# Interleaving the first gate and up weight quarters of a two-layer hybrid decoder step, and storing its last two output tiles singly

## The reference

```
x <- LN1(alpha*x + 0.5*SwiGLU_1(x))
x <- LN2(alpha*x + W_o( sum_b sigmoid(g_b(x)) * y_b(x) ))
x <- LN3(alpha*x + 0.5*SwiGLU_2(x))
_swiglu(x, wg, wu, wd) = (silu(x @ wg) * (x @ wu)) @ wd        # D_FF = 2816
```

## Time and profile before

| | |
|---|---|
| median of 3 runs | 1395.87 us (1395.16 to 1395.97) |
| the profiled execution | 1396.94 us, of which its span is 1395.0 us |
| instructions | 25447 |
| PE busy | 1376.8 us (99%), 10566 matmuls |
| DVE busy | 898.0 us (64%) |
| ACT busy | 667.2 us (48%) |

### The profile page before, as it was taken

The page is one execution under the profiler, slowest core; times in us unless marked ns, Lnnn a source line. Parts: engine busy times, 40 slices in busy tenths (PEclk is TensorE's granted clock), DMA queues, the critical chain, the costliest instruction groups (busy, mean ns, idle before and its releaser), DMA issues.

```text
span 1395.0 us, 25447 instructions
## 1 busy us (share of the span) xinstructions
PE 1376.8 (99%) x10566; PEld 1356.7 (97%) x10566; DVE 898.0 (64%) x1180; ACT 667.2 (48%) x896; POOL 35.0 (3%) x68
## 2 busy tenths in 40 slices
PE   8999999999999999999999999999999999999996
PEld 8999999999899999999999999999998999999996
DVE  5555558486965885554685555686887568655444
ACT  5444446445444664444474444463544355644433
POOL 0100000000101000000000000000001000000000
PEclk9999999999999999999999999999999999999999
DMA  6554444654656454444445544445465453554441
GB/s 237 204 180 155 148 167 164 223 181 172 232 190 212 162 182 160 170 158 161 166 167 179 180 156 149 166 165 198 166 240 197 166 201 122 181 180 153 171 166 57
DMA packets 39997, 243.60 MB, mean 175 GB/s; under 512 B 4576, under 2 KB 4592, under 8 KB 16368
## 3 DMA queue, kind: packets, MB, share of 16 engines
q1 hardware_dynamic: 33264, 219.00, 45.2%
q0 software_dynamic: 5936, 22.01, 4.3%
q10 hardware_dynamic: 720, 1.47, 0.3%
HBM read 238.97 MB, written 3.50 MB: 174 GB/s over the span
## 4 chain that ended last, share of the span: by engine, by line
PE 92%; DVE 5%; DMA 1%; ACT 1%; issue 1%; DVEq 0%
PE ps L438 29%; PE ps L437 29%; PE ps L439 29%; DVE wlo L1026 1%; DMA raw<-in_w_in 1%; PE ps L525 1%; PE ps L629 1%; PE ps L652 1%; PE ps L597 0%; PE ps L636 0%; ACT whi L729 0%; PE ps L469 0%; DMA raw<-in_ffn_wg 0%; PE ps L470 0%; PE ps L474 0%
## 5 line engine op out<-in xcount | busy, mean ns | idle before, releaser
L1026 DVE TENSOR_TENSOR wlo<-raw,whi 128x1024 fp32r<-128x1024 f32 (+1 forms) x450 | 510.4, 1141 | 314.6 <-ACT whi L729 310.7
L729 ACT CAST whi<-raw 128x1024 fp32r<-128x1024 f32 (+1 forms) x446 | 438.1, 987 | 496.5 <-PE ps L439 397.6
L437 PE MATMUL ps<-xh,whi 128*128 128x288 f32 (+1 forms) x2144 | 635.9, 297 | 1.2 <-DVE xl L1225 1.2
L438 PE MATMUL ps<-xl,whi 128*128 128x288 f32 (+1 forms) x2144 | 631.4, 294 | 0.0
L439 PE MATMUL ps<-xh,wlo 128*128 128x288 f32 (+1 forms) x2144 | 630.5, 294 | 0.0
L437 PEld LDWEIGHTS ps<-xh,whi 128*128 128x128 f32 x2144 | 404.5, 189 | 3.6 <-DVE xl L1225 1.6
L438 PEld LDWEIGHTS ps<-xl,whi 128*128 128x128 f32 x2144 | 406.2, 189 | 0.8
L439 PEld LDWEIGHTS ps<-xh,wlo 128*128 128x128 f32 x2144 | 405.5, 189 | 0.0
L437 PE MATMUL ps<-hh,whi 128*128 128x288 f32 (+1 forms) x1088 | 322.2, 296 | 0.0
L438 PE MATMUL ps<-hl,whi 128*128 128x288 f32 (+1 forms) x1088 | 319.4, 294 | 0.0
L439 PE MATMUL ps<-hh,wlo 128*128 128x288 f32 (+1 forms) x1088 | 319.2, 293 | 0.0
(11 more groups left out here) (185 smaller groups left out, 750.5 us busy)
## 6 DMA issues: line engine op xcount, KB each, us to landing
raw<-in_w_in SPq DMA_DIRECT2D x48, 1024.0 KB, 4.9
raw<-in_ffn_wg SPq DMA_DIRECT2D x43, 1024.0 KB, 4.9
raw<-in_ffn_wu SPq DMA_DIRECT2D x43, 1024.0 KB, 4.8
raw<-in_ffn_wd SPq DMA_DIRECT2D x32, 1024.0 KB, 4.9
raw<-in_ffn_wd SPq DMA_DIRECT2D x16, 768.0 KB, 4.2
pool<-in_cache_k POOLq DMA_DIRECT2D x16, 512.0 KB, 4.3
pool<-in_cache_v POOLq DMA_DIRECT2D x16, 512.0 KB, 6.2
raw<-in_w_o SPq DMA_DIRECT2D x8, 1024.0 KB, 4.9
```

The lines of the kernel that those rows point to most:

```text
L437: mm(out, wh, mh, start=start, stop=False)
L438: mm(out, wh, ml, start=False, stop=False)
L729: s_.copy(whi[:, s, k0:k1, :], raw[:, s, k0:k1, :]).then_inc(hi_ready, 1)
L1026: return v.tensor_tensor(out, full, high.bitcast(F32), sub)
```

## The change

It does five things.

1. SP issues the two first blocks by turns in quarters: gate 0, up 0, gate 1, up 1 and so on, 8 issues of 256 KB in place of 4 of 256 KB and 2 of 512 KB. Each up quarter has a semaphore of its own (`second_in`).
2. ACT no longer casts the first x quarter; DVE does (`first_xh`). ACT casts gate quarter c, x quarter c (from c = 1) and up quarter c by turns; DVE computes `wlo` of the gate quarter, `xl`, and `wlo` of the up quarter by turns.
3. PE multiplies gate quarter c and then up quarter c. Within a quarter it does the four `whi*xh` matmuls, the four `wlo*xh` and the four `whi*xl`. From c = 1 the first of them waits for `xl` and `wlo` of the quarter as well. `pe_half` is counted behind gate quarters 1 and 3, and twice behind up quarter 3.
4. The 16 matmuls on zeros are all 256 columns wide.
5. SP stores output pairs 0-1, 2-3, 4-5 and then tile 6 alone; ACT stores tile 7 alone.

POOL's code is unchanged, and so is everything from block 2 on.

```diff
-WARM_NARROW, WARM_WIDE = 8, 8
+WARM = 16
...
-                        src = I["ffn1_wg"][0, 0]
-                        for c, full in enumerate((*first_in, raw_full[0])):
-                            sp.dma_start(raw[:, 0, 2 * c:2 * c + 2, :], src[:, 2 * c:2 * c + 2, :]).then_inc(full, 16)
-                        src = I["ffn1_wu"][0, 0]
-                        for (k0, k1), full in zip(halves(KD), (second_in, raw_full[1])):
-                            sp.dma_start(raw[:, 1, k0:k1, :], src[:, k0:k1, :]).then_inc(full, 16)
+                        for c, full in enumerate(zip((*first_in, raw_full[0]), (*second_in, raw_full[1]))):
+                            for s, w in enumerate(("ffn1_wg", "ffn1_wu")):
+                                sp.dma_start(raw[:, s, 2 * c:2 * c + 2, :],
+                                             I[w][0, 0][:, 2 * c:2 * c + 2, :]).then_inc(full[s], 16)
...
-            for p in range(PAIRS_D - 1):
-                sp.wait_ge(x_full, KD * (3 * L - 1) + min(2 * p + 2, ENDS_ON_ACT))
-                if 2 * p + 2 > ENDS_ON_ACT:
-                    sp.wait_ge(y_last, 2 * p + 2 - ENDS_ON_ACT)
-                sp.dma_start(O["y"][:, 2 * p:2 * p + 2, :], x[:, 2 * p:2 * p + 2, :]).then_inc(y_out, 16)
+            def leave(k0, k1):
+                sp.dma_start(O["y"][:, k0:k1, :], x[:, k0:k1, :]).then_inc(y_out, 16)
+
+            for k0, k1 in ((0, 2), (2, 4), (4, 6), (6, 7)):
+                sp.wait_ge(x_full, KD * (3 * L - 1) + min(k1, ENDS_ON_ACT))
+                if k1 > ENDS_ON_ACT:
+                    sp.wait_ge(y_last, k1 - ENDS_ON_ACT)
+                leave(k0, k1)
...
+            def first_blocks():
+
+                for c in range(PAIRS_D):
+                    for s in range(2):
+                        if (s, c) == (0, 0):
+                            pe.wait_ge(first_xh, 1)
+                            pe.wait_ge(first_hi, 1)
+                        for part in range(3):
+                            if s == 0:
+                                if part == 1:
+                                    pe.wait_ge(lo_ready if c % 2 else first_lo, c // 2 + 1)
+                                if part == 2 or (c > 0 and part == 0):
+                                    pe.wait_ge(x_ready, 2 * c + 2)
+                                if c > 0 and part == 0:
+                                    pe.wait_ge(lo_ready if c % 2 else first_lo, c // 2 + 1)
+                            elif part == 0:
+                                if c < PAIRS_D - 1:
+                                    pe.wait_ge(second_lo, c + 1)
+                                else:
+                                    pe.wait_ge(lo_ready, 4)
+                            w = wlo if part == 1 else whi
+                            for k in (2 * c, 2 * c + 1):
+                                m = xl[:, k, :] if part == 2 else xh[:, k, :]
+                                for t in range(2):
+                                    last = mm(ps[:, 2 * s + t, 0:T], w[:, s, k, t * P:(t + 1) * P], m,
+                                              start=k == 0 and part == 0, stop=k == KD - 1 and part == 2)
+                        if (s, c) in ((0, 1), (0, PAIRS_D - 1)):
+                            last.then_inc(pe_half, 1)
+                        elif (s, c) == (1, PAIRS_D - 1):
+                            last.then_inc(pe_half, 2)
...
-                act.wait_ge(x_in[c], 16)
-                s_.copy(xh[:, p, :], x[:, p, :]).then_inc(xh_ready, 2)
-            for (k0, k1), full in zip(halves(KD), (second_in, raw_full[1])):
-                act.wait_ge(full, 16)
-                split(1, 1, k0, k1)
+                if c > 0:
+                    act.wait_ge(x_in[c], 16)
+                    s_.copy(xh[:, p, :], x[:, p, :]).then_inc(xh_ready, 4 if c == 1 else 2)
+                act.wait_ge((*second_in, raw_full[1])[c], 16)
+                hi_part = s_.copy(whi[:, 1, p, :], raw[:, 1, p, :])
...
-                        s_.dma_start(O["y"][:, KD - 2:KD, :], x[:, KD - 2:KD, :]).then_inc(y_out, 16)
+                        s_.dma_start(O["y"][:, KD - 1:KD, :], x[:, KD - 1:KD, :]).then_inc(y_out, 16)
...
+            dve.wait_ge(x_in[0], 16)
+            v.tensor_copy(xh[:, 0:2, :], x[:, 0:2, :]).then_inc(first_xh, 1)
             for c in range(PAIRS_D):
                 p = slice(2 * c, 2 * c + 2)
                 dve.wait_ge(hi_ready if c % 2 else first_hi, c // 2 + 1)
                 rest(wlo[:, 0, p, :], raw[:, 0, p, :], whi[:, 0, p, :]).then_inc(lo_ready if c % 2 else first_lo, 1)
-                dve.wait_ge(x_in[c], 16)
-                dve.wait_ge(xh_ready, 2 * c + 2)
+                if c == 0:
+                    dve.wait_ge(first_xh, 1)
+                else:
+                    dve.wait_ge(x_in[c], 16)
+                    dve.wait_ge(xh_ready, 2 * c + 2)
                 rest(xl[:, p, :], x[:, p, :], xh[:, p, :]).then_inc(x_ready, 2)
-            for h in range(2):
-                lo(1, h)
+                if c < PAIRS_D - 1:
+                    dve.wait_ge(second_hi, c + 1)
+                else:
+                    dve.wait_ge(hi_ready, 4)
+                lo_part = rest(wlo[:, 1, p, :], raw[:, 1, p, :], whi[:, 1, p, :])
+                if c < PAIRS_D - 1:
+                    lo_part.then_inc(second_lo, 1)
+                else:
+                    lo_part.then_inc(lo_ready, 2)
```

## The result

The changed kernel takes **1402.2 us** (median of 6 runs, 1400.73 to 1403.46) against 1395.92 us for the kernel before, measured beside it (6 runs, 1394.98 to 1398.16). The ratio is 1.0041, with a 95% interval from 1.003 to 1.0051: slower by 0.4%, 6.3 us where the forecast had 2.7, and outside its range, which ended at 1400.5. The profiled execution took 1401.38 us, with a span of 1399.6.

The account below looks back on a forecast made before the run. PE was taken to bound the kernel, without slack behind block 2. Block 2's delay through the parameters, +2.7 us, with nought for start and stores, was added to 1395.87 us: 1398.6 us, range 1397.2 to 1400.5.

Parts of the forecast that it names:

- The landing of the quarters: Start: interleaved weight quarters land from 5.8 to 13.0 us; gate 1 comes 1.7 us later, gate 3 2.0 us later.
- that rival: Start: quarters flow slower, gate 3 lands at 14.7, everything 1.5 us later, 1400.1 us; chance 8%.
- ACT, DVE and the issues: First blocks: last xl ends at 15.30, 2.8 us later; block 2's load issued at 14.75, parameters at 15.96, block 3's at 16.1.
- the view that block 2 hangs on the parameters: Before block 2: last xl, 0.65 us to POOL, 4.5 us load, 3.5 us on ACT and DVE release it; slack nil.
- the landing of the parameters: Before block 2: parameters issued at 15.96 land after 4.5 us as before, at 20.45.
- The rival of the fallen clock: PE's new 3.2 us pause: clock falls, block 2 starts at 0.24 us a matmul, 1400.0 to 1402 us; chance 10%.
- the forecast's chain: Before block 2: later last xl delays parameters, then 3.5 us on ACT and DVE; block 2 at 23.9 for 21.19, +2.7 us.
- a sign of being wrong: After the pause: matmuls of 0.24 us would show the forecast wrong.
- the price stated: After PE's pause: a fallen clock costs 1.3 to 3.4 us more.
- The start's gain: Blocks 0 and 1: PE ends 0.5 to 0.7 us earlier but then waits, so no gain; rival that it stands, 1395.3 us, 8%.
- The stores: End of kernel: splitting the last stores could save up to 0.3 us or cost 0.35 us; taken as nought.
- no slack that could take up a delay: Between block 2 and the last LayerNorm: PE entering block 2 later moves the end by the same time.

Follow-up runs that it names:

- the start alone: Kernel before with 16 wide zero matmuls, DVE's first x cast and whi*xh first; loads and parameters in their old places: 1396.65 us, ratio 1.0003.
- the second profile: The kernel after, unchanged, measured and profiled again beside later experiments: 1403.87 us, ratio 1.005.
- the kernel before with late parameters: Kernel before with one wait added on POOL, so parameters load when wlo of both first blocks is done: 1403.68 us, ratio 1.0064.
- the kernel with block 3's load behind: Kernel after, but SP issues block 3's load only when the parameters have landed: 1401.56 us, ratio 1.0043; a second profiled execution took 1400.05 us.

## Why the prediction was wrong, point by point

**The landing of the quarters was right.** I had 5.8, 7.3, 9.0, 10.4 and 11.1 for the first five; ACT's casts began at 6.1, 7.4, 9.1, 10.5 and 11.3. Gate 3 landed at 12.6 (issued at 3.71, 8.9 us to landing), where the forecast had 12.4 and the rival 14.7; the last quarter landed at 13.2, for 13.0. So the small transfers did not flow more slowly, and that rival did not come. The rule in the Trainium skill (DMA: Bandwidth & Descriptors, section Bandwidth) to batch into 1 MiB or more, given there with figures of transfers issued from GpSimd, did not show in these eight queued ones.

**ACT, DVE and the issues were right to 0.1 us or so.** The last xl ended at 15.27 (15.30), SP's load of block 2 went at 14.78 (14.75), POOL's at 15.91 (15.96), block 3's at 15.89 (16.1). So was the view that block 2 hangs on the parameters: the two kernels in which only their load was moved show it from both sides, the start alone from a third.

**The step that failed is the landing of the parameters.** I kept 4.5 us because "The distance between the two loads stays 1.2 us, so they share the DMA engines as before". That distance did stay (1.21 us before, 1.13 after), and the landing did not. What I left out is block 3's load. It came 2.2 us behind the parameters before (15.38 for 13.18) and went out with them after (15.89 for 15.91). I had both times, and wrote of block 3's only that it is needed late. The term was 6.8 us, in the second profile 7.8, sized as 4.5: +2.3 to +3.3 us. Taking block 3's load away brought it to 5.5, not to 4.5. So 1.3 to 2.3 us of the error are block 3's load, and the cause of the last 1.0 us stays open. The chain behind it kept its length (3.5 us from 22.84 to 26.30).

**The rival of the fallen clock came true, on top of the forecast's chain.** I gave it 10% because a pause of 3.2 us had to be enough, and I had one fall, 4.5 us after the last matmul. The pause was 5.2 us. Two errors hung together: with the landing right, the clock's fall would have been the likely case, at 1398.6 + 2.3 + 2.5 = 1403.4. But the 10% was also low for a pause of 3.2 us. The six falls near the pause, in the traces of the kernel after and of the experiments, came 2.7 to 5.3 us after PE's last matmul in blocks 0 and 1, so the 4.5 us of one trace were no measure for the next. The matmuls of 0.24 us after the pause, named as a sign of being wrong, came, and the price stated (1.3 to 3.4 us) held the 2.5 us of the trace. All pauses from 3.85 us on had a fall, 1.7 us had none, and a pause filled with matmuls on zeros had none. A pause of 3.2 us was not tried.

**The start's gain** was there in the profile, 0.4 us at the first matmul, and hidden, as said. It isn't steady: in the six other traces with interleaved loads the first real matmul comes at 6.79 to 7.29, for 7.29 to 7.35 in the three with the old start. The wide matmuls on zeros may have helped with the clock: full pace sets in between 6.2 and 9.2 us in the ten traces that have them, between 8.6 and 10.0 in the three that don't. PE was done with the two blocks at 21.2, not at 20.7 to 20.9: it took 0.135 us a matmul there, for 0.132 before. **The stores** brought nothing, as said.

**One reading was incomplete.** The earlier trace rows shows one of three waits of PE behind the start. The same view has a longer one, here before and after:

```profile
PE ps L643 <- DVE pool L1448: 1.9, 2, 1.1
PE ps L651 <- DVE pool L1472: 0.9, 2, 0.5
```

So "no slack that could take up a delay" was not quite true: 0.9 us of the delay were gone behind these two waits. That they are shorter because PE comes later is not shown; in the second profile of the kernel after they take 2.0 us.

## What to carry to other kernels

When work is put earlier, list what is issued behind it on every queue, an idle engine's too, and lay the new issue times side by side: a small load that goes out together with large ones lands late (here after 6.3 to 7.8 us, for 2.9 with nothing beside it), so its old landing time holds only among its old neighbours. A load on which a whole engine waits in program order belongs where the queues are quiet, and ahead of its need. And give a new pause of PE a price for the clock as well, unless it is no longer than one that is known to have left the clock full: here pauses of 3.85 to 6.2 us cost 1.5 to 2.5 us more than their length.

## What the runs showed of the hardware that I had not expected

**The clock can fall after the pause.** In the kernel before with late parameters PE was at work again from 24.82, and the clock went to half near 26.3 for 3.4 us; in the kernel after it fell within the pause (near 25.1) and stayed down until 31.9. In the kernel with block 3's load behind, it fell 2.7 us after PE's last matmul in one execution and 5.1 us after it in the other. The same pause costs differently from execution to execution.

**The matmul pace inside a loop has a few levels.** At a granted clock of 1.00, and with PE never idle, the first loop takes 0.13167 us a matmul in the kernel before, 0.13055 in the profiled run of the kernel after, 0.13222 in its second one. Here are 100 us of it in these three, in that order:

```profile
60.00:160.00 100.00, 100.00 (x762) 100.00 (x761) 54.98 (x55) 42.73 (x49) 0.00 (x0) 1.00 0.49 169
```

```profile
60.00:160.00 100.00, 100.00 (x769) 100.00 (x768) 56.57 (x56) 44.06 (x50) 1.13 (x2) 1.00 0.52 180
```

```profile
60.00:160.00 100.00, 100.00 (x758) 100.00 (x758) 55.94 (x56) 43.33 (x50) 1.83 (x3) 1.00 0.51 176
```

The same three values turn up in all thirteen traces, in one loop this, in another that, with no relation to an edit that I can see: each loop of about 1000 matmuls is thereby up to 1.7 us faster or slower. This is what gave the kernel after some 2 of the 3 us back in its profile (matched matmul by matmul it is 7.6 us late at 34 us, 6.0 at 250, 5.0 at 600, 5.9 at 950 and 4.5 at the end); the other 0.9 us are the shorter waits for DVE named above. It may also be behind much of the scatter of the kernel before, from 1391.1 to 1400.2 us, but with one trace of that kernel this is not shown. What sets the level is open; no run tested it.
